# The chunked scan of a hybrid diffusion block: X and Y of a step in four transfers, k k whole, the block inverse in rectangles, the router on column groups

## The chip, the cores and the metric

One Trainium2 chip, one of its cores. The metric is the device time of one execution in microseconds, median of three. All data is fp32.

## The reference

One layer over 1024 latent tokens and 256 context tokens, width 1024. Modulated RMS norm, one input projection, a depthwise convolution, then a token mixer with two head groups, each run forwards and backwards: a gated DeltaNet with 4 heads of 128 x 128 and a Mamba-2 SSD with 8 heads. The context is scanned first, and the latent scan starts from its last state. Then gated norms and the output projection, a second norm, and an expert-choice mixture of 16 SwiGLU experts. The parts that the change touches are these:

```python
# DeltaNet, per chunk
lmat = jnp.where(strict, jnp.einsum("cbhid,cbhjd->cbhij", kb, kc) * decay, 0.0)
uw = lax.linalg.triangular_solve(lmat + jnp.eye(CHUNK, dtype=lmat.dtype), rhs,
                                 left_side=True, lower=True, unit_diagonal=True)
v_new = u_i - jnp.einsum("bhld,bhdv->bhlv", w_i, S)
o = jnp.einsum("bhld,bhdv->bhlv", qg_i, S) + jnp.einsum("bhij,bhjv->bhiv", qk_i, v_new)
S = S * jnp.exp(gl_i)[..., None, None] + jnp.einsum("bhld,bhlv->bhdv", kt_i, v_new)
...
# router of the experts
aff = jax.nn.softmax(jnp.einsum("btd,de->bte", h, router_w).astype(jnp.float32), axis=-1)
gate, idx = lax.top_k(jnp.swapaxes(aff, 1, 2), cap)
```

## The kernel before

Five engines run programs written out by hand, with semaphores between them. In order of time:

- **Projection and convolution** (to about 550 us). 26 blocks of 128 output columns pass through TensorE (L1874) and the convolution on VectorE (L2241). Products k k per tile of 128 tokens go to `kk_dram`, q k to `qk_dram`. The diagonal 32 x 32 blocks of the triangular matrix are inverted in a batch; X (the inverses) and Y (the inverses times beta, transposed) of every tile, head and direction go to `xy_dram`.
- **The scan** (about 555 to 765 us). 20 steps, direction and tile alternating: step s is direction s % 2, n = s // 2; the first four are context steps, the other 16 latent steps. A tile is 128 tokens. In step s every engine works on three steps at once: `own` (s), `nxt` (s + 1) and `two` (s + 2).
- **The merge** (about 772 to 953 us). Eight tiles of 128 tokens: both directions are summed and normed, turned, multiplied with the output projection (L1078), normed again to h2, turned (L1048) and multiplied with the router's weights (`router`, L1057).
- **The choice of rows** (to about 1000 us), then **the experts** (to 1285 us, L1115 and L1134) and the final norm and add.

One step of the scan on TensorE: `from_k(own)`, `block_w(nxt)`, `from_state(own)`, `solve(own)`, `block_vy(nxt)`, `from_chunk(own)` (L495), `outputs(own)` (L468, L469), `block_vp(nxt)`, `to_s(own)`, `to_state(own)`, `block_vq(nxt)`. All seven DeltaNet products but `outputs` go through `per_head` (L411): four heads, 128 x 128 by 128 x 128 each. L484 is `from_state`, L505 `to_state`.

The inverse of the whole 128 x 128 triangle is put together from the four diagonal blocks of X by four of these products, in PSUM bank bA of the direction: W = AT x X, copied to SBUF by ScalarE (L574); P = Y - W x Y on VectorE (`block_p`, L630); Q = W x P, copied by ScalarE; Y += W x Q on VectorE (`block_y`, L635). AT is k k times the decay E, made by VectorE (`block_a`, L625) in place in a buffer per direction, which the load has filled in three rectangles around the diagonal blocks.

VectorE's order in a step: `rest(own)` (L640), `scores(own)` (L686), the mask of E (L606), `y_off` (L670), `block_p(nxt)`, the mask of the SSM decay (L606, wide), `y_diag` (L677), `block_a(two)`, `new_s(own)` (L650), `new_hs(own)` (L662), `block_y(nxt)`. ScalarE's: copy of W, copy of U, exponentials of E (L538), `scaled_x` (L559), copy of Q, exponentials of the SSM decay (L550), copy of the outputs (L600), `tail_k` (L568). GpSimd's: `query_e` (q k x E, L741), `with_eg` (L725, L727), `decayed_hs` (L735), `tail_x` (L748).

SyncE issues all loads of the scan in one order. In step s: `load_at(two)` (L804), `load_xy(two)` (L815), `load_kg(two)` (eg, L822), `load_e(three)` (g, L792), `load_e8(two)` (L830), `load_qk(two)` (L837), `load_kt(two)` (L843), then the store of the outputs of `own` (L889). An issue waits for the buffer that it fills, and all behind it wait too. Behind the scan, SyncE loads the first two tiles of the merge (L979, L982) once GpSimd has made the last product with k (L727).

## Time and profile before

| | |
|---|---|
| median of three executions | 1387.87 us (1385.27 to 1390.42) |
| the profiled execution | 1388.71 us, span 1387.0 us |
| TensorE busy | 1245.3 us, 90% of the span |
| VectorE busy | 764.1 us, 55% |
| ScalarE busy | 430.8 us, 31% |
| GpSimd busy | 220.3 us, 16% |
| mean granted TensorE clock | 0.953 of full speed |

TensorE is PE in the rows, its weight loads PEld, VectorE DVE, ScalarE ACT, GpSimd POOL, SyncE SP. A q behind the name is the engine's queue of DMA issues. Busy time on PE counts a matmul from start to end although the next one has begun; the distance of starts tells what one costs. In brackets behind a row stands the engine's idle time before it and what released it.

### The profile page before, as it was taken

Reading aid. Unit: us, or ns where it says so; the run is one execution under the profiler, and the core shown is the slowest. Engines: PE = TensorE matmul, PEld = TensorE weight load, DVE = VectorE, ACT = ScalarE, POOL = GpSimd, SP = SyncE. Lnnn points to the kernel's source line nnn. Section 1 sums busy time; section 2 is a strip of 40 time slices with the busy share of each in tenths; the row PEclk is TensorE's granted clock in tenths of the full one; section 3 lists DMA queues with packets and bytes.
Section 4 is the critical chain, followed back from the end, with each engine's and each line's share of the span. In section 5 each row is a group of like instructions: output and inputs, shape, how many; then the busy total and the mean of one; then the engine's idle time right before and its main releaser. Section 6 shows DMA issues by size and latency. Waiting matters only on the chain.

```text
span 1387.0 us, 14619 instructions
## 1 busy us (share of the span) xinstructions
PE 1245.3 (90%) x5410; PEld 733.2 (53%) x5410; DVE 764.1 (55%) x1110; ACT 430.8 (31%) x1094; POOL 220.3 (16%) x206
## 2 busy tenths in 40 slices
PE   4999999999999998899999689992199999999983
PEld 3455555455455555889999345552044444444441
DVE  5199889887927776598887446546601101010124
ACT  6233232313111114677786243432011010110122
POOL 0300000010000031266665000000101011010112
PEclk9899999999999999999999799995599999999996
DMA  9823454552052451567676724426479999999967
GB/s 365 265 77 98 125 157 139 158 164 92 17 167 50 106 110 29 149 180 218 206 211 207 260 91 182 181 77 245 149 273 318 350 330 340 333 330 349 320 226 161
DMA packets 207532, 270.69 MB, mean 195 GB/s; under 512 B 75053, under 2 KB 124198, under 8 KB 207462
## 3 DMA queue, kind: packets, MB, share of 16 engines
q1 hardware_dynamic: 187118, 210.97, 46.8%
q0 software_dynamic: 14272, 52.43, 12.6%
q10 hardware_dynamic: 6072, 6.35, 1.3%
q8 instruction: 43, 0.70, 0.2%
q14 instruction: 27, 0.22, 0.1%
HBM read 217.75 MB, written 51.97 MB: 194 GB/s over the span
## 4 chain that ended last, share of the span: by engine, by line
PE 66%; DVE 13%; DMA 10%; ACT 4%; issue 3%; SPq 3%; POOL 0%; POOLq 0%; ACTq 0%; DVEq 0%
PE ps L1874 23%; PE ps L1115 13%; PE ps L411 7%; PE ps L1134 6%; DVE arena L2241 3%; PE ps L1078 2%; DMA y_dram<-arena 2%; DMA arena<-zt_dram 2%; DMA tok_dram<-arena 2%; DMA arena<-ada_w 2%; PE ps L1773 1%; PE ps L495 1%; PE ps L468 1%; PE ps L469 1%; PE ps L1104 1%
## 5 line engine op out<-in xcount | busy, mean ns | idle before, releaser
L1874 PE MATMUL ps<-arena 128*128 128x512 f32 (+1 forms) x1072 | 423.4, 552 | 0.0
L1874 PEld LDWEIGHTS ps<-arena 128*128 128x128 f32 x1072 | 201.3, 190 | 199.5 <-issue 194.4
L1115 PE MATMUL ps<-arena 128*128 128x512 f32 x512 | 226.8, 596 | 1.4 <-ACT arena L1238 1.4
L2241 DVE SCALAR_TENSOR_TENSOR arena<-arena,taps 128x1024 f32<-128x1024 f32 x160 | 209.3, 1308 | 5.5
L1115 PEld LDWEIGHTS ps<-arena 128*128 128x128 f32 x512 | 96.5, 191 | 116.8 <-issue 114.8
L411 PE MATMUL ps<-arena 128*128 128x128 f32 x1080 | 132.2, 277 | 9.7 <-DVE arena L630 4.2
L411 PEld LDWEIGHTS ps<-arena 128*128 128x128 f32 x1080 | 127.2, 192 | 15.8 <-DVE arena L630 5.2
L1401 DVE TENSOR_TENSOR arena<-arena,ps 128x512 f32<-128x512 f32 x16 | 11.0, 688 | 224.1 <-PE ps L1115 224.1
L1078 PE MATMUL ps<-arena 128*128 128x512 f32 x256 | 116.0, 608 | 4.2 <-ACT arena L1187 4.2
L1134 PE MATMUL ps<-arena 128*128 128x512 f32 x256 | 112.8, 593 | 0.0
L1078 PEld LDWEIGHTS ps<-arena 128*128 128x128 f32 x256 | 48.6, 194 | 62.3 <-issue 56.2
L1134 PEld LDWEIGHTS ps<-arena 128*128 128x128 f32 x256 | 47.8, 191 | 55.2 <-issue 55.2
L1258 ACT ACTIVATE arena<-ps 128x512 f32<-128x512 f32 x16 | 9.6, 597 | 198.7 <-PE ps L1115 198.7
L1474 POOL DMA_INDIRECT y_dram<-arena x14 | 22.3, 1593 | 290.5 <-DVE arena L1411 290.5
L2056 ACT ACTIVATE arena<-arena,vcols 128x1280 f32<-128x1280 f32 (+1 forms) x20 | 25.9, 1297 | 136.7 <-DVE arena L2241 136.6
L1238 ACT ACTIVATE arena<-ps 128x512 f32<-128x512 f32 x32 | 19.0, 595 | 144.3 <-PE ps L1104 144.3
L1410 DVE TENSOR_SCALAR arena<-ps,arena 128x512 f32<-128x512 f32 x15 | 11.3, 751 | 91.7 <-PE ps L1134 91.7
L2257 DVE SCALAR_TENSOR_TENSOR arena<-arena,silu_c 128x256 f32<-128x256 f32 x112 | 56.9, 508 | 4.0
L1681 POOL DMA_DIRECT2D arena<-ada_w x16 | 14.5, 906 | 264.5 <-DVE arena L2257 218.0
L574 ACT ACTIVATE arena<-ps 128x512 f32<-128x512 f32 x60 | 35.5, 591 | 51.3 <-PE ps L411 50.8
L606 DVE TENSOR_TENSOR arena<-arena,neg_mask 128x512 f32<-128x512 f32 (+1 forms) x36 | 40.0, 1113 | 5.9 <-DMA arena<-g_dram 5.8
L756 POOL TENSOR_TENSOR arena<-arena,gates 128x1280 f32<-128x1280 f32 x4 | 10.0, 2501 | 205.1 <-DVE arena L2241 185.5
(314 smaller groups left out, 1536.1 us busy)
## 6 DMA issues: line engine op xcount, KB each, us to landing
arena<-exp_w_gate SPq DMA_DIRECT2D x16, 2048.0 KB, 11.0
arena<-exp_w_up SPq DMA_DIRECT2D x16, 2048.0 KB, 9.1
arena<-exp_w_down SPq DMA_DIRECT2D x16, 2048.0 KB, 11.2
arena<-ada_w POOLq DMA_DIRECT2D x16, 1024.0 KB, 6.6
arena<-w_in SPq DMA_DIRECT2D x28, 512.0 KB, 4.7
arena<-ada_w SPq DMA_DIRECT2D x4, 2048.0 KB, 19.9
arena<-x SPq DMA_DIRECT2D x16, 512.0 KB, 6.6
arena<-g_dram SPq DMA_DIRECT2D x16, 512.0 KB, 6.2
```

Source lines behind the costliest of these rows:

```text
L411: last = mm(out[:, h * P:(h + 1) * P], lhsT[:, h, :], rhs[:, h, :], start=True, stop=True)
L574: a(flat(dst), src[:], ACT.Copy).then_inc(sem(name), 1)
L606: return nc.vector.tensor_tensor(out, out, bh(neg_mask[:, d, :], n), ALU.add)
L1078: last = mm(ps[2 + 2 * s + h][:], mixT[s][:, k, :], wo[:, k, h * 512:(h + 1) * 512], start=(k == 0), stop=(k == KD - 1))
L1115: last = mm(ps[gu_bank[s] + j][:], xsT[s][:, k, :], ew[s][j][:, k, :], start=(k == 0), stop=(k == KD - 1))
L1134: last = mm(ps[4 + h][:], hidT[s][:, k, :], ew[s][2][:, k, h * 512:(h + 1) * 512], start=(k == 0), stop=(k == KF - 1))
L1238: a(xsT[e % 2][:, 4 * h:4 * h + 4, :], heads(ps[0][:]), ACT.Copy).then_inc(sem("xsT"), 1)
L1474: p.indirect_dma_start(y_dram, bass.IndirectOffsetOnAxis(ap=idxT[:, e:e + 1], axis=0), ye[e % 2], None, compute_op=ALU.add).then_inc(sem(" ...
L1874: last = mm(ps[3 * (m % 2) + gi][:, 0:w], wring[(m + 1) % NW][:, k, :], hT[:, k, o:o + w], start=(k == 0), stop=(k == KD - 1))
L2056: ins = a(dst, cacc[n_conv(mm) % 2][:, 0:w], ACT.Silu, bias=bcol)
L2241: ins = v.scalar_tensor_tensor(accg, cin_l[ci % 2][:, j // 3:j // 3 + GR, j % 3:j % 3 + GW], tp[:, j:j + 1], accg, ALU.mult, ALU.add)
L2257: ins = v.scalar_tensor_tensor(out, blk[:, k, :], silu_c[:, k, 0:1], out, ALU.mult, ALU.add)
```

## The change

**X and Y.** `xy_dram` is laid out by direction, tile and then X or Y. A step's X and Y come in four transfers (one for each block row) in place of eight.

**k k.** The whole product of a tile (128 x 512) is loaded in one transfer into one buffer KK, shared by all steps. `block_a` multiplies it with E in three rectangles, writing AT. AT is never filled by a load any more. The load for a step waits until the multiply of the step before has read KK.

**The inverse in rectangles.** W, Q and the last product are made, copied and added only in the rectangle where they are not zero: W of direction 1 in rows 0 to 95 and columns 32 to 127, Q in rows 0 to 95 and one half of the columns, the last product in 64 rows and 64 columns. The contraction leaves out rows in which W is zero. Direction 0's W stays whole.

**The router on column groups.** The router's weights, padded to 32 columns a block, are stationary, the transposed h2 moves, and block k writes to rows 32 (k % 4) on, so four sums of two blocks each stand in one bank; the first sum is put in the middle of the first half of the output projection. ScalarE copies them (`logit_parts`), and one matmul with a folded identity adds them (`router_sum`). VectorE builds the padded weights and the folded identity at the start of the merge.

The diff, cut to its core:

```diff
-    xy_dram = dram("xy_dram", (2, 2, NT, DN_H, NB, BL * BL))
+    xy_dram = dram("xy_dram", (2, NT, 2, DN_H, NB, BL * BL))
...
+        KK = zero
...
+        HI, TOP = slice(P // 2, P), slice(0, P - BL)
+        W_R = ((slice(0, P), slice(0, P)), (TOP, slice(BL, P)))
+        Q_R = ((TOP, HI), (TOP, slice(0, P // 2)))
+        Y_R = ((slice(0, P // 2), HI), (HI, slice(0, P // 2)))
...
+            def in_region(d, rc, lhsT, rhs, k=slice(0, P)):
+
+                rows, cc = rc
+                for h in range(DN_H):
+                    last = mm(heads(bA[d][:])[rows, h, cc], lhsT[k, h, rows], rhs[k, h, cc], start=True, stop=True)
+                return last
...
-                per_head(bA[d], AT[d], Xd[d]).then_inc(sem("s_blk"), 1)
+                in_region(d, W_R[d], AT[d], Xd[d]).then_inc(sem("s_blk"), 1)
...
-                per_head(bA[d], W[d], Yd[d]).then_inc(sem("s_blk"), 1)
+                in_region(d, (slice(0, P), slice(0, P)), W[d], Yd[d], W_R[d][0]).then_inc(sem("s_blk"), 1)
...
-                per_head(bA[d], W[d], Y[d]).then_inc(sem("s_blk"), 1)
+                in_region(d, Q_R[d], W[d], Y[d], W_R[d][0]).then_inc(sem("s_blk"), 1)
...
-                per_head(bA[d], W[d], Q[d]).then_inc(sem("s_blk"), 1)
+                in_region(d, Y_R[d], W[d], Q[d], TOP).then_inc(sem("s_blk"), 1)
...
             def block_a(step):
                 d, n = step
-                dve.wait_ge(sem(f"ld_at{d}"), 48 * (n + 1))
+                dve.wait_ge(sem("ld_kk"), 16 * turn(d, n + 1))
                 dve.wait_ge(sem("s_ee"), turn(d, n + 1))
-                v.tensor_tensor(AT[d], AT[d], e_of(step), ALU.mult).then_inc(sem("s_at"), 1)
+                if n > 0:
+                    dve.wait_ge(sem("s_blk"), part(4, (d, n - 1), 1))
+                else:
+                    dve.wait_ge(sem("zero"), 3 + DN_H)
+                kk, e = heads(KK), e_of(step)
+                for b in range(NB - 1):
+                    rows = slice(BL * (b + d), BL * (b + d + 1))
+                    cc = slice(BL * (b + 1), P) if d == 0 else slice(0, BL * (b + 1))
+                    last = v.tensor_tensor(AT[d][rows, :, cc], kk[rows, :, cc], e[rows, :, cc], ALU.mult)
+                last.then_inc(sem("s_at"), 1)
...
+                y_ = region(Y[d], Y_R[d])
+                v.tensor_tensor(y_, y_, region(heads(bA[d][:]), Y_R[d]), ALU.add).then_inc(sem("s_py"), 1)
...
+            p.memset(W[1][:, :, 0:BL], 0.0).then_inc(sem("zero"), 1)
...
+            def load_kk(step):
+                d, n = step
+                if step != steps[0]:
+                    sp_.wait_ge(sem("s_at"), turn(d, n + 1) - 1)
+                sp_.dma_start(KK, kk_dram[tile_of(step)]).then_inc(sem("ld_kk"), 16)
...
-                for dst, x_ in ((Xd[d], 0), (Yd[d], 1)):
-                    xy = xy_dram[d, x_, t].rearrange("h b (j i) -> b j h i", i=BL)
-                    for b in range(NB):
-                        rows = slice(BL * b, BL * (b + 1))
-                        sp_.dma_start(dst[rows, :, rows], xy[b]).then_inc(sem(f"ld_xy{d}"), 16)
+                src = xy_dram[d, t].rearrange("x h b (j i) -> b j (x h) i", i=BL)
+                for b in range(NB):
+                    rows = slice(BL * b, BL * (b + 1))
+                    sp_.dma_start(XY[d][rows, :, rows], src[b]).then_inc(sem(f"ld_xy{d}"), 16)
...
-            load_at(steps[0])
-            load_at(steps[1])
+            sp_.wait_ge(sem("aux"), AUX[("late", 3, 0)] + 1)
+            load_kk(steps[0])
...
             load_xy(steps[1])
+            load_kk(steps[1])
...
-                    load_at(two)
+                    load_kk(two)
                     load_xy(two)
...
                 for k in range(KD):
-                    last = mm(ps[1][:, 0:E_N], h2T[s][:, k, :], rw[:, k, :], start=(k == 0), stop=(k == KD - 1))
+                    rows = slice(BL * (k % NB), BL * (k % NB + 1))
+                    last = mm(ps[1][rows, 0:P], rwide[:, k, :], h2T[s][:, k, :], start=(k < NB), stop=(k >= KD - NB))
                 last.then_inc(sem("logit"), 1)
+
+            def router_sum(t):
+                pe.wait_ge(sem("lparts"), t + 1)
+                mm(ps[1][:, P:P + E_N], lparts[t % 2], fold2[:, 0:E_N], start=True, stop=True).then_inc(sem("lsum"), 1)
...
+            def logit_parts(t):
+                act.wait_ge(sem("logit"), t + 1)
+                if t >= 2:
+                    act.wait_ge(sem("lsum"), t - 1)
+                a(lparts[t % 2], ps[1][:, 0:P], ACT.Copy).then_inc(sem("lparts"), 1)
...
+            v.memset(rwide[:, :, E_N:BL], 0.0)
+            v.tensor_copy(rwide[:, :, 0:E_N], rw[:])
+            link(v.tensor_tensor(fold2, ident[:, 0:BL], ident[:, BL:2 * BL], ALU.add))
+            for q in range(2, NB):
+                link(v.tensor_tensor(fold2, fold2, ident[:, q * BL:(q + 1) * BL], ALU.add))
```

ScalarE's copies of W and Q take the same rectangles, and the stores into `xy_dram` follow its new layout.

## Rows read from the trace of the kernel before

**Rows 1.** The page: busy tenths and granted clock in 40 slices.
```profile
PE   4999999999999998899999689992199999999983
PEclk9899999999999999999999799995599999999996
```
**Rows 2.** Busy time by stretch (PE, PEld, DVE, ACT, POOL, clock, DMA): context, 14 latent steps.
```profile
555.00:594.00 39.00, 32.86 (x258) 30.70 (x256) 22.45 (x35) 24.41 (x67) 12.19 (x10) 1.00 0.62 167
...
599.81:755.60 155.79, 155.55 (x1571) 148.44 (x1570) 131.68 (x211) 121.88 (x391) 96.40 (x69) 1.00 0.66 200
```
**Rows 3.** TensorE's timeline in one latent step: start, duration, line, shapes.
```profile
661.79 2.02 PE L411 MATMUL ps<-arena 128*128 128x128 f32 x16
663.74 1.15 PE L495 MATMUL ps<-arena 128*64 128x64 f32 x32
...
666.71 1.95 PE L411 MATMUL ps<-arena 128*128 128x128 f32 x16
668.50 1.03 PE L505 MATMUL ps<-arena 128*128 128x256 f32 x4
669.37 2.84 PE L411 MATMUL ps<-arena 128*128 128x128 f32 x24
...
672.96 2.02 PE L411 MATMUL ps<-arena 128*128 128x128 f32 x16
```
**Rows 4.** Who waited for whom, 600 to 755 us: total, times, longest.
```profile
POOL arena L741 <- DMA arena<-qk_dram: 48.5, 13, 5.3
...
DVE arena L662 <- POOL arena L735: 10.1, 11, 1.2
```
**Rows 5.** The context steps: chain of waits, then TensorE's timeline.
```profile
580.17 6.81 DMA arena<-qk_dram
```
```profile
591.37 2.05 PE L411 MATMUL ps<-arena 128*128 128x128 f32 x16 [2.01 <-POOL arena L727]
```
**Rows 6.** Chain of waits at a router product; weight loads by shape.
```profile
926.43 1.69 PE ps L1057 x16
```
```profile
L411 PEld LDWEIGHTS ps<-arena 128*128 128x128 f32 x1080 | 127.2, 192 | 15.8 <-DVE arena L630 5.2 <-issue 4.7 <-POOL arena L727 2.2
...
L495 PEld LDWEIGHTS ps<-arena 128*64 128x64 f32 x512 | 16.3, 138 | 2.5 <-issue 0.9
```
**Rows 7.** VectorE's timeline: the multiply before the scan and in it.
```profile
545.15 0.69 DVE L625 TENSOR_TENSOR arena<-arena 128x512 f32<-128x512 f32 x1
...
667.43 1.26 DVE L625 TENSOR_TENSOR arena<-arena 128x512 f32<-128x512 f32 x1 [1.05 <-DMA arena<-kk_dram]
...
678.61 1.25 DVE L625 TENSOR_TENSOR arena<-arena 128x512 f32<-128x512 f32 x1 [1.06 <-DMA arena<-kk_dram]
```
**Rows 8.** SyncE's queue of issues in one latent step.
```profile
668.13 0.43 SPq L837 DMA_DIRECT2D arena<-qk_dram  x1
...
671.24 0.32 SPq L889 DMA_DIRECT2D scan_dram<-arena  x1
671.61 2.13 SPq L804 DMA_DIRECT2D arena<-kk_dram  x3
673.78 4.62 SPq L815 DMA_DIRECT2D arena<-xy_dram  x8
```
**Rows 9.** DMA issues: count, size, median us to landing; then q k's.
```profile
arena<-kt_dram SPq DMA_DIRECT2D x18, 256.0 KB, 6.6
```
```profile
DMA to landing us min/median/max: 3.2/6.5/8.1
```
**Rows 10.** The end of the scan: GpSimd's and VectorE's timelines.
```profile
753.66 2.13 POOL L727 TENSOR_TENSOR arena<-arena 128x512 f32<-128x512 f32 x1
```
```profile
772.25 0.19 DVE L1277 TENSOR_TENSOR mods<-mods,vcols 128x32 f32<-128x32 f32 x1 [9.14 <-DMA scan_dram<-arena]
```
**Rows 11.** Chain of waits in the merge: a middle tile, the last router product.
```profile
836.72 6.13 DMA arena<-zt_dram
...
949.13 3.61 PE ps L1057 x16
```

More of the change, by code:

```diff
@@ L400, in pe_first @@
             pe.wait_ge(sem("s_at"), 1)
-            pe.wait_ge(sem("ld_xy0"), 128)
+            pe.wait_ge(sem("ld_xy0"), 64)
             for h in range(DN_H):
@@ L581, in act_scan @@
                     d, n = nxt
-                    evac(bA[d], W[d], nxt, ("s_blk", part(4, nxt, 1)), "s_wq")
+                    evac(region(heads(bA[d][:]), W_R[d]), region(W[d], W_R[d]), nxt, ("s_blk", part(4, nxt, 1)), "s_wq")
                 if own:
                     d, n = own
-                    evac(bB[d], U[d], own, ("s_xr", turn(d, n + 1)), "s_u")
+                    evac(heads(bB[d][:]), U[d], own, ("s_xr", turn(d, n + 1)), "s_u")
                 if own and two:
@@ L591, in act_scan @@
                     d, n = nxt
-                    evac(bA[d], Q[d], nxt, ("s_blk", part(4, nxt, 3)), "s_wq")
+                    evac(region(heads(bA[d][:]), Q_R[d]), region(Q[d], Q_R[d]), nxt, ("s_blk", part(4, nxt, 3)), "s_wq")
                 if lat(nxt):
@@ L634, in block_y @@
                 dve.wait_ge(sem("s_blk"), part(4, step, 4))
-                v.tensor_tensor(Y[d], Y[d], heads(bA[d][:]), ALU.add).then_inc(sem("s_py"), 1)
+                y_ = region(Y[d], Y_R[d])
+                v.tensor_tensor(y_, y_, region(heads(bA[d][:]), Y_R[d]), ALU.add).then_inc(sem("s_py"), 1)
             def rest(step):
@@ L793, in load_e @@
                     .then_inc(sem(f"ld_e{d}"), 16)
-            def load_at(step):
+            def load_kk(step):
                 d, n = step
-                t = tile_of(step)
-                if n > 0:
-                    sp_.wait_ge(sem("s_blk"), part(4, (d, n - 1), 1))
-                kk = kk_dram[t].rearrange("p (h n) -> p h n", h=DN_H)
-                for b in range(NB - 1):
-                    rows = slice(BL * (b + d), BL * (b + d + 1))
-                    cc = slice(BL * (b + 1), P) if d == 0 else slice(0, BL * (b + 1))
-                    sp_.dma_start(AT[d][rows, :, cc], kk[rows, :, cc]).then_inc(sem(f"ld_at{d}"), 16)
+                if step != steps[0]:
+                    sp_.wait_ge(sem("s_at"), turn(d, n + 1) - 1)
+                sp_.dma_start(KK, kk_dram[tile_of(step)]).then_inc(sem("ld_kk"), 16)
             def load_xy(step):
@@ L922, in hybrid_block @@
         lmax = take(NL)
+        rwide = take(KD * BL).rearrange("p (k n) -> p k n", k=KD)
+        lparts = [take(P) for _ in range(2)]
+        fold2 = take(BL)
         at[0] = 0
@@ L1079, in pe_tail @@
                                   start=(k == 0), stop=(k == KD - 1))
-                    if h == 0 and t >= 2:
-                        router(t - 2)
+                        if h == 0 and k == 3 and t >= 2:
+                            router(t - 2)
+                        if h == 1 and k == 3 and t >= 2:
+                            router_sum(t - 2)
                 last.then_inc(sem("mps"), 1)
@@ L1085, in pe_tail @@
                 router(t)
+                router_sum(t)
             pe.wait_ge(sem("route"), 2)
@@ L1227, in act_tail @@
                     back_sum(t - 1)
+                if t >= 2:
+                    logit_parts(t - 2)
+                if 1 <= t <= NL:
                     back_x2(t - 1)
```

17 lines of the change are left out of this document (10 added, 7 removed).

## The prediction

> **What bounds the kernel now.** I read the page's slices first, to find the stages, then busy time by stretch, then each engine's timeline over one step of the scan, then the chain of waits on both sides of it. The slices [rows 1] show TensorE nearly full and at full clock from the second slice to about 770 us; the clock falls only around 770 us and from 940 to 1000 us. The change touches two places: the scan (555 to 765 us) and the merge with the router (772 to 953 us).
>
> In the latent part of the scan TensorE is the bound: busy 155.55 of 155.79 us in fourteen steps [rows 2], 11.13 us each. A step on TensorE's timeline [rows 3], from 661.79 to 672.96 us, is 56 instructions of the per-head helper (an fp32 matmul is two), 32 of the chunk product, 16 of the outputs and eight wide ones, back to back. Two gaps come from it: 128 moving columns cost (668.50 - 666.71)/16 = 112 ns each, 256 columns (669.37 - 668.50)/4 = 218 ns, so 0.83 ns a column plus 6. But others are close behind [rows 4]: GpSimd idles 48.5 us on the load of q k, VectorE 10.1 us on GpSimd, and about 1.05 us a step on the load of k k [rows 7]. Walking the step, new_hs ends some 0.4 us before TensorE asks for it, and the solve has about 0.1 us to spare behind the same GpSimd work. So a shorter TensorE step is worth its full amount only if q k lands earlier too.
>
> The four context steps are different: TensorE is busy 32.86 of 39 us [rows 2], and the chain of waits runs through SyncE's queue, eight issues of X and Y, the G load behind them, the q k load at 580.17, and GpSimd, until from_k starts after 2.01 us of idle at 591.37 [rows 5].
>
> **The inverse in rectangles.** It removes columns of W (direction 1), P, and Q. P's product has 96 stationary and 64 moving columns, the last product 64 and 64, W of direction 1 96 and 96. What is the gap of such a pair? Moving columns alone give 58 ns at 64 and 85 at 96. But the router's old matmuls, 128 stationary and 16 moving, still take 1.69/16 = 106 ns [rows 6]: there the weight load sets the gap. Its duration is 192 ns at 128 columns and 138 at 64 [rows 6], 0.84 ns a column, so I take 106 - 27 = 79 ns at 96 and 52 at 64. The larger of the two sides gives P 79, the last product 58, W 85. Savings: 8 x (112 - 79) = 0.26 us, 8 x 54 = 0.43 us, 8 x 27 = 0.22 us. Direction 0 gains 0.69 us a step, direction 1 0.91. The first step's inverse is serial and then waits for the G load, so it counts nothing: 9 x 0.69 + 10 x 0.69 + 9 x 0.22 = **15.1 us**. Bounds: if 96 weight columns cost as 128 do, P gains 0.05 us instead of 0.26 and the total is 11.1; if weights don't count at these widths, P gains 0.43 and the total is 18.3.
>
> The Trainium skill ("TensorE: Matmul & The Clock Gate", part 3, The mechanism) says that a weight load overlaps a running matmul only when it targets another row group. All the rectangles use the same row groups, so by that rule nothing overlaps. The trace disagrees: serial, 128 columns would take at least 106 + 106 ns and take 112. The same page (LDWEIGHTS) gives P/1.2 ns for P stationary columns, 80 ns at 96 and 53 at 64; by it the sum would be 15 us, mine.
>
> ScalarE's copies shrink too (W by a quarter in direction 1, Q by half), and VectorE's last add falls from 128x512 to 64x256: about 0.25 us each, off the path in the latent steps.
>
> **k k whole, and the multiply in three.** AT = k k x E was one VectorE instruction on 512 columns, 0.68 us alone and 1.25 us when GpSimd works beside it [rows 7]. Now it is three of 384, 256 and 128 columns. At 0.6 us of work for 512 columns plus 0.06 to 0.15 us an instruction that is 1.1 to 1.25 us alone, up to 2.0 beside GpSimd. With the 0.27 us that the last add gives back, VectorE gets 0.2 to 0.5 us more on some 9.4 of 11.13 us [rows 2]. I expect 9.7 of 10.35: it fits, with the waits inside it. I charge **1.0 us** over the scan; bounds 0 and 0.45 us a latent step, 7 us.
>
> The wait is new: there is one k k buffer, so a load goes out only once the multiply before it is done. On SyncE it stands behind the output store, which goes out after the outputs' copy; at that moment the multiply has long ended (668.70 against 671.61) [rows 7, 8]. So the semaphore costs nothing in a latent step; the bytes may. Before, three issues took from 671.61 to 673.75 and the multiply started at 678.61 after 1.06 us of idle. Now one issue of 0.43 us moves 256 KB right behind the store's 512 KB. The nearest rows are kt, of the same 256 KB, median 6.6 us to landing, and q k, 3.2 to 8.1 us [rows 9]. VectorE gets to the multiply some 5.5 us after the issue and has about 1.5 us of reserve before the next solve. So landing below 7 us costs nothing, and I take 5.5. In the context steps the round trip (0.43 + about 4 + 1.2 us) stays under the step of 7.4 us. At the start the second k k waits for the first multiply (545.15 + 1.2 us) and goes out behind X and Y at about 548, well before its use some 9 us after the first multiply: nothing.
>
> **X and Y in four.** An issue costs about 0.49 us on SyncE's queue whatever its shape: eight take from 673.78 to 678.45 [rows 8]. Four fewer, and two k k issues fewer, take 3.3 to 4 us from SyncE in every step. Everything behind (eg, G, the G of the SSM heads, q k) goes out earlier. q k waits for the outputs of its direction, behind which the next block starts at 666.71 [rows 3], and was issued at 668.13 only because the queue was behind, so it gains 1.1 us there, and more in landing since 512 KB before it have already moved. GpSimd's chain thus stays ahead of a TensorE step 0.8 us shorter. That is what lets the 15.1 us count. The context part gains the stalls: 2.0 us at 591.37 [rows 5], 0.2 right behind it, and 0.3 in the steps before, where VectorE's mask of G stood ahead of P: **2.5 us**; bounds 1 and 4.
>
> **Behind the scan** the tail's loads (4 MB) start when GpSimd's last k multiply ends at 755.8, and the merge starts 16.4 us later [rows 10]. q k earlier moves that multiply some 1 us more than TensorE's end: **1.0 us**; bounds 0 and 2.5.
>
> **The router.** On four column groups, 32 stationary columns each, sixteen instructions should take about 0.6 us: the chunk product on two groups takes 1.15 us for 32 [rows 3]. It adds a ScalarE copy (0.3 us), one matmul for the fold and the hops between. In the middle tiles the path is the load of z transposed, VectorE and ScalarE [rows 11], and TensorE waits: nothing. On the last tiles it is on the path: 926.43, 1.69 us become 0.6 + 0.2, saves 0.9; 949.13, 3.61 us at half clock become about 1.15 + 0.5 (copy) + 0.65 (fold) + 0.2, saves 1.1. Against it VectorE builds the padded router weights and the fold before the first tile, five small instructions of 0.19 to 0.23 us [rows 10], 1.05 us on the path. Net **1.0 us**; bounds -1 and 2. The new store layout of X and Y moves the same rows of 4 KB: nothing.
>
> **Sum.** 15.1 - 1.0 + 2.5 + 1.0 + 1.0 = 18.6 us. The profiled execution took 1388.71 us (span 1387.0); less 18.6 is 1370.1. The median of the three runs is 0.84 lower, so I predict **1369.3 us**.
>
> **Rivals.**
> - *VectorE or GpSimd becomes the bound.* For it: VectorE was busy or waiting on GpSimd nearly all of a step, and the multiply runs beside GpSimd. Against it: 2.2 us of its idle go when q k and k k land earlier. A latent step of about 10.8 us: 16 x 0.45 = 7 us back, 1376.5 us.
> - *Wide weights hold P.* The 96-column load costs as 128: 4 us back, 1373.5. Its opposite, no weight limit: 1366.
> - *Slower: k k lands late.* One buffer, the load can't start before the store's wait is over. It begins to cost at 7 us from issue to landing, and each us more is a us on every one of the 16 latent steps. Half a per cent slower needs (18.6 + 6.9)/16 = 1.6 us more, 8.6 us; at 9 us it is 32 us against the 18.6, 1401 us. For it: q k, of the same size, has landed as late as 8.1 us [rows 9]. Against it: that was behind 1.3 MB issued within 2 us, k k stands behind 0.75 MB.
> - *Little or nothing.* From a step's outputs over q k, GpSimd, new_hs, the last add and the solve to the outputs two steps on is a ring of two steps, 22.3 us with 0.1 to spare. If q k lands no earlier, only the smaller add shortens it: 21.9 us, 10.95 a step, 0.6 x 16 = 9.6 us back, 1378.9. With a costlier multiply in the same ring, as in the first rival, it passes 1381.
>
> **How the numbers follow.** Forecast 0.58, its own range 1366 to 1373; VectorE or GpSimd the bound 0.17; weights otherwise, outside that range, 0.12; little or nothing 0.08; late k k 0.05. The range runs from all low costs together but one (1361) to the little-or-nothing case (1379.5). Half a per cent, 6.9 us, is about what tells a change from none here: below 1381 it is faster, 0.87, within 0.08, slower 0.05.
>
> **What would show it.** Right: a latent step of 10.2 to 10.5 us with TensorE still full; blocks of the last product at 0.46 us; the load of q k no longer what GpSimd waits longest for; from_k of the first latent step without idle; four issues in 2 us. Wrong: VectorE idle on k k over 1.5 us a step; TensorE idle on VectorE before P or the solve; the P block still 0.9 us.

## The result, and the profile after

The changed kernel takes 1394.48 us (median of 11 runs, 1392.55 to 1399.37) against 1389.65 us (11 runs of the kernel before beside it, 1382.93 to 1392.97). The ratio is 1.0038 with a 95% interval of 1.0022 to 1.0054: 5 us slower, where 18.6 us faster was forecast. The profiled execution has a span of 1392.6 us and a granted clock of 0.951. Of all the executions in this document one, of kernel 10, ran at a lower granted clock (0.914) and took 1420.43 us; it is left out of the median there.

I split the difference of 5.6 us between the two spans at four marks that both traces have: the start of the first P on VectorE, of the last from_state on TensorE, of VectorE's first instruction of the merge, and of its search for the largest logit.

| mark (us) | before | after | step longer by |
|---|---|---|---|
| first P | 553.7 | 559.5 | +5.8 |
| last from_state | 759.0 | 766.4 | +1.6 |
| merge starts | 772.3 | 779.1 | -0.6 |
| largest logit | 953.0 | 959.2 | -0.6 |

Behind the last mark the changed kernel is 0.6 us shorter. So the net loss is what was lost ahead of the scan, and the scan itself, where 16.6 us were to come from, is 1.6 us longer.

**Ahead of the scan.** Busy time by stretch, one stretch over the stores of X and Y and the next: the last two columns are the DMA engines' busy share and GB/s. First the kernel before, then the changed one.
```profile
380.00:385.00 5.00, 5.00 (x13) 2.24 (x12) 1.69 (x3) 0.00 (x0) 0.00 (x0) 1.00 0.53 166
385.00:390.00 5.00, 5.00 (x19) 2.58 (x18) 0.00 (x0) 2.17 (x4) 0.00 (x0) 1.00 1.02 339
```
```profile
380.00:385.00 5.00, 5.00 (x13) 2.18 (x12) 1.25 (x3) 0.00 (x0) 0.00 (x0) 1.00 0.27 48
385.00:390.00 5.00, 5.00 (x19) 2.64 (x18) 0.00 (x0) 2.17 (x4) 0.00 (x0) 1.00 0.50 181
```
And of the changed kernel the chain of waits, then who waited for whom from 400 to 470 us on TensorE.
```profile
390.03 20.11 DMA arena<-w_in
```
```profile
PE ps L1924 <- DMA arena<-w_in: 4.9, 1, 4.9
```
The same eight stores, of the same bytes, keep the DMA engines half as busy. The first load of projection weights is issued behind them, takes 20.11 us to land, and TensorE stands still for 4.9 us. The kernel before has no such wait: it reached the same projection with its weights in place. From the issue of the first of these stores to the first P it is 178.4 us in the changed kernel and 172.1 before. Over all the traces of this case it is 172.0 to 173.6 us in the eight kernels with the old layout and 178.4 to 179.2 in the five with the new one (kernel 12, which cuts some stores up, stands apart), so the layout costs 6 to 7 us.

**A latent step.** TensorE's timeline of the changed kernel over one step, which answers to [rows 3].
```profile
661.21 0.81 PE L441 MATMUL ps<-arena 128*96 128x64 f32 x8
661.87 1.11 PE L422 MATMUL ps<-arena 128*128 128x128 f32 x8
662.81 1.03 PE L525 MATMUL ps<-arena 128*128 128x256 f32 x4
663.77 0.68 PE L441 MATMUL ps<-arena 96*64 96x64 f32 x8
664.38 1.16 PE L422 MATMUL ps<-arena 128*128 128x128 f32 x8
665.37 0.84 PE L441 MATMUL ps<-arena 128*96 128x96 f32 x8
666.05 1.06 PE L504 MATMUL ps<-arena 128*128 128x256 f32 x4
667.53 1.13 PE L422 MATMUL ps<-arena 128*128 128x128 f32 x8 [0.42 <-DVE arena L670]
```
Read the distances of starts, not the durations. P's product takes 661.87 - 661.21 = 0.66 us for eight, 82 ns each (79 forecast). W of direction 1 takes 666.05 - 665.37 = 0.68, 85 ns (85 forecast). The last product takes 664.38 - 663.77 = 0.61, 76 ns (58 forecast), and the full-width block behind it 0.99 instead of the 0.90 of eight at 112 ns. The four wide ones ahead of it (L525, before L505) take 663.77 - 662.81 = 0.96 us where they took 0.87 [rows 3]. The last line is new: TensorE waits on VectorE.

Over 120 us of the latent part, busy time of PE, PEld, DVE, ACT and POOL: before, then after.
```profile
620.00:740.00 120.00, 119.98 (x1201) 114.42 (x1198) 99.53 (x162) 94.70 (x304) 76.09 (x55) 1.00 0.70 211
```
```profile
620.00:740.00 120.00, 113.35 (x1186) 104.03 (x1185) 118.93 (x179) 89.35 (x296) 77.89 (x53) 1.00 0.73 218
```
The bound has changed hands. TensorE was full and has 6.65 us of idle now; VectorE is full. The mean distance of thirteen latent steps, from from_state to from_state, went from 11.12 to 11.34 us; some steps take 10.6, others 12.3.

Where TensorE idles tells what holds it. Its waits in this window, then its timeline at one of them:
```profile
PE ps L515 <- issue: 5.3, 7, 1.0
```
```profile
681.36 1.15 PE L515 MATMUL ps<-arena 128*64 128x64 f32 x32 [0.73 <-issue]
```
The profile names no releaser, but L515 is the chunk product, which waits for VectorE's scores (L716). In each of its eight waits in this window it starts 0.10 us after the second scores product has ended. So 5.4 of TensorE's 6.65 us of idle are a wait for the scores.

What fills VectorE stands in its instructions by shape in the same window (busy us, mean ns of one, idle before). Before, then after:
```profile
L686 DVE TENSOR_TENSOR arena<-arena 128x512 f32<-128x512 f32 x22 | 14.2, 684 | 0.0
L625 DVE TENSOR_TENSOR arena<-arena 128x512 f32<-128x512 f32 x11 | 13.5, 1228 | 7.2 <-DMA arena<-kk_dram 7.2
...
L606 DVE TENSOR_TENSOR arena<-arena,neg_mask 128x512 f32<-128x512 f32 x10 | 6.8, 685 | 0.0
```
```profile
L716 DVE TENSOR_TENSOR arena<-arena 128x512 f32<-128x512 f32 x22 | 28.7, 1342 | 0.0
L626 DVE TENSOR_TENSOR arena<-arena,neg_mask 128x512 f32<-128x512 f32 x11 | 15.8, 1433 | 0.0
...
L659 DVE TENSOR_TENSOR arena<-arena,ps 128x512 f32<-128x512 f32 x11 | 7.4, 672 | 0.0
...
L653 DVE TENSOR_TENSOR arena<-arena 32x384 f32<-32x384 f32 x10 | 6.0, 596 | 0.1
L653 DVE TENSOR_TENSOR arena<-arena 32x256 f32<-32x256 f32 x10 | 5.1, 514 | 0.1
L665 DVE TENSOR_TENSOR arena<-arena,ps 64x256 f32<-64x256 f32 x11 | 4.6, 414 | 0.2
L653 DVE TENSOR_TENSOR arena<-arena 32x128 f32<-32x128 f32 x10 | 3.6, 357 | 0.2
```
The multiply in three (1.47 us) is hardly dearer than the one was (1.23). The scores (L716, before L686) and the narrow mask (L626, before L606), which the change doesn't touch, take twice as long: 1342 and 1433 ns against 684 and 685. An instruction of the same size with one operand from PSUM (L659) keeps its 672. The two timelines show it; VectorE's, then GpSimd's:
```profile
677.77 0.69 DVE L670 TENSOR_TENSOR arena<-arena,ps 128x512 f32<-128x512 f32 x1
678.38 2.88 DVE L716 TENSOR_TENSOR arena<-arena 128x512 f32<-128x512 f32 x2
681.18 1.52 DVE L626 TENSOR_TENSOR arena<-arena,neg_mask 128x512 f32<-128x512 f32 x1
682.63 0.68 DVE L700 TENSOR_TENSOR arena<-ps,eG 128x512 f32<-128x512 f32 x1
```
```profile
677.76 1.28 POOL L755 TENSOR_TENSOR arena<-arena 128x512 f32<-128x512 f32 x1
679.11 1.59 POOL L757 TENSOR_TENSOR arena<-arena 128x512 f32<-128x512 f32 x1
680.67 1.49 POOL L765 TENSOR_TENSOR arena<-arena,eGt 128x512 f32<-128x512 f32 x1
682.12 1.49 POOL L778 TENSOR_TENSOR arena<-arena,wtail 128x512 f32<-128x512 f32 x1
```
In these rows a VectorE instruction with both operands in SBUF takes about as long as the GpSimd product beside it (1.44 and 1.52 us against 1.28 to 1.59); those with one operand from PSUM keep their 0.68 and 0.69 us. That is contention, not work: run 3 below, which takes GpSimd's work away, brings the scores back to 693 and the narrow mask to 700 ns. The Trainium skill ("SBUF — State Buffer", Who interferes with whom) says that a VectorE instruction with two SBUF inputs contends with a GpSimd instruction that reads SBUF, while one with at most one SBUF input does not. The rows agree with it on both sides.

**Queue and loads.** SyncE's queue of issues in a latent step answers to [rows 8]; under it the DMA issues of the scan (count, KB, median us to landing), which answer to [rows 9].
```profile
666.52 0.43 SPq L830 DMA_DIRECT2D arena<-kk_dram  x1
666.99 2.36 SPq L840 DMA_DIRECT2D arena<-xy_dram  x4
...
672.64 0.32 SPq L862 DMA_DIRECT2D arena<-qk_dram  x1
```
```profile
arena<-kk_dram SPq DMA_DIRECT2D x14, 256.0 KB, 3.6
...
arena<-qk_dram SPq DMA_DIRECT2D x14, 256.0 KB, 3.9
```
k k whole lands in 3.6 us, X and Y go out in 2.36, and q k is issued 0.2 us behind the outputs (672.45) instead of 1.4, and lands in 3.9. This part did what was forecast, but for one sign: GpSimd still waits longest for the load of q k, 46.3 us between 620 and 740 (before: 41.2), since its issue waits for the outputs.

**The scan's end and the merge.** GpSimd's last k product, VectorE's first instruction of the merge [rows 10], and the chain at a middle and at the last router product [rows 11]:
```profile
758.33 2.49 POOL L757 TENSOR_TENSOR arena<-arena 128x512 f32<-128x512 f32 x1
```
```profile
779.09 0.19 DVE L1322 TENSOR_TENSOR mods<-mods,vcols 128x32 f32<-128x32 f32 x1 [8.58 <-DMA scan_dram<-arena]
```
```profile
931.50 0.57 PE ps L1086 x16
...
939.13 0.13 PE ps L1091 x2
...
956.84 1.12 PE ps L1086 x16
...
958.32 0.62 PE ps L1091 x2
```
The merge starts 18.3 us behind GpSimd's last product (16.4 before). A router product costs 0.57 + 0.13 us instead of 1.69, the last one 2.1 from first matmul to fold instead of 3.61.

### The profile page after: what moved, and what is told of

It reads as the page before. It is cut to its first block, busy times and chain, and to the rows that moved or that the text cites. A ratio compares the mean times of both kernels' runs of the same rounds, so it can differ in the third digit from the quotient of the medians.

```text
span 1392.6 us, 14592 instructions
## 1 busy us (share of the span) xinstructions
PE 1235.7 (89%) x5426; PEld 711.5 (51%) x5426; DVE 792.7 (57%) x1155; ACT 426.7 (31%) x1102; POOL 226.0 (16%) x207
## 4 chain that ended last, share of the span: by engine, by line
PE 53%; DVE 25%; DMA 9%; ACT 5%; issue 5%; SPq 2%; POOLq 0%; DVEq 0%; ACTq 0%
PE ps L1924 21%; PE ps L1151 13%; PE ps L1170 6%; DVE arena L626 3%; DVE arena L716 3%; PE ps L1111 2%; DMA y_dram<-arena 2%; DVE arena L2291 2%; DMA arena<-ada_w 2%; DVE arena L2362 1%; DVE arena L2360 1%; DMA arena<-w_in 1%; DMA arena<-zt_dram 1%; PE ps L1823 1%; PE ps L441 1%
## 5 line engine op out<-in xcount | busy, mean ns | idle before, releaser
L1924 PEld LDWEIGHTS ps<-arena 128*128 128x128 f32 x1072 | 201.9, 191 | 206.1 <-issue 195.9
L1151 PEld LDWEIGHTS ps<-arena 128*128 128x128 f32 x512 | 96.7, 192 | 117.2 <-issue 115.1
L1111 PEld LDWEIGHTS ps<-arena 128*128 128x128 f32 x256 | 47.9, 194 | 60.0 <-issue 54.0
L441 PE MATMUL ps<-arena 128*128 128x128 f32 (+5 forms) x632 | 71.2, 257 | 6.8 <-DVE arena L659 3.9
L1170 PEld LDWEIGHTS ps<-arena 128*128 128x128 f32 x256 | 48.1, 192 | 55.6 <-issue 55.6
L441 PEld LDWEIGHTS ps<-arena 128*128 128x128 f32 (+4 forms) x632 | 64.0, 172 | 14.4 <-issue 7.8
L1303 ACT ACTIVATE arena<-ps 128x512 f32<-128x512 f32 x16 | 9.6, 598 | 199.2 <-PE ps L1151 199.2
L422 PE MATMUL ps<-arena 128*128 128x128 f32 x448 | 63.5, 285 | 3.2 <-DVE arena L670 2.6
L1283 ACT ACTIVATE arena<-ps 128x512 f32<-128x512 f32 x32 | 19.0, 594 | 144.3 <-PE ps L1140 144.3
L422 PEld LDWEIGHTS ps<-arena 128*128 128x128 f32 x448 | 55.9, 194 | 8.0 <-DVE arena L665 3.5
L626 DVE TENSOR_TENSOR arena<-arena,neg_mask 128x512 f32<-128x512 f32 (+1 forms) x36 | 48.4, 1346 | 2.6 <-DMA arena<-g_dram 2.6
## 6 DMA issues: line engine op xcount, KB each, us to landing
arena<-exp_w_gate SPq DMA_DIRECT2D x16, 2048.0 KB, 11.1
```

Source lines behind the costliest of these rows:

```text
L422: last = mm(out[:, h * P:(h + 1) * P], lhsT[:, h, :], rhs[:, h, :], start=True, stop=True)
L441: last = mm(heads(bA[d][:])[rows, h, cc], lhsT[k, h, rows], rhs[k, h, cc], start=True, stop=True)
L626: return nc.vector.tensor_tensor(out, out, bh(neg_mask[:, d, :], n), ALU.add)
L1111: last = mm(ps[2 + 2 * s + h][:], mixT[s][:, k, :], wo[:, k, h * 512:(h + 1) * 512], start=(k == 0), stop=(k == KD - 1))
L1151: last = mm(ps[gu_bank[s] + j][:], xsT[s][:, k, :], ew[s][j][:, k, :], start=(k == 0), stop=(k == KD - 1))
L1170: last = mm(ps[4 + h][:], hidT[s][:, k, :], ew[s][2][:, k, h * 512:(h + 1) * 512], start=(k == 0), stop=(k == KF - 1))
```

## The experiments

Each was run against the kernel before on the same chip. "Step" is the mean distance of thirteen latent steps (before: 11.12 us), VectorE's and TensorE's busy time is of the 120 us from 620 to 740. Times of different runs come from different chips, so each is compared with the kernel before beside it.

**1. The old store layout in the changed kernel** (with it X and Y need eight loads again)
```diff
-xy_dram = dram("xy_dram", (2, NT, 2, DN_H, NB, BL * BL))
+xy_dram = dram("xy_dram", (2, 2, NT, DN_H, NB, BL * BL))
```


> The changed kernel with X and Y as before: the old layout of xy_dram, stores of 128 rows at one stride, eight loads a step. Theory A (the new store layout is slow and holds up the load of w_in behind it, and in the scan VectorE and GpSimd bound each other): the load of w_in that landed 20.1 us after 390.03 lands in about 14, the scan starts 5 to 6 us earlier, and the latent steps stay near 11.4 us, since the four issues are not what makes them long: about 1388 us. Rival B (four transfers in place of eight moved q k early, and that shifted GpSimd onto VectorE's SBUF work): the latent steps fall to 11.1 us or less as well, about 1384. Rival C (the late start comes from elsewhere): the start of the scan does not move, 1394.

1391.98 us, ratio 1.0024 (1.0002 to 1.0046). The first P starts at 551.4, 8 us earlier (of which 1.7 lie ahead of the stores), and the stall on w_in is gone. But the step is 11.41 us and VectorE busy 118.84. The layout costs its microseconds ahead of the scan, and X and Y in four have nothing to do with the long steps.

**2. query_e held back until P's copy is there**
```diff
                 pool.wait_ge(sem("s_ee"), turn(d, n + 1))
+                pool.wait_ge(sem("s_py"), part(2, step, 1))
```


> The changed kernel, but GpSimd's q k times E of the next step waits until VectorE has written P of that step, so that GpSimd's five products begin about 4 us later in the step, beside VectorE's reads of PSUM and not beside the scores and the narrow mask. Theory A (contention between the two on SBUF, by phase): the scores fall from 1.35 us each to 0.75, the narrow mask from 1.47 to 0.75, latent steps to 10.6 to 10.8 us, in all 8 to 12 us faster than the changed kernel, about 1384. Rival D (VectorE has simply too much to do with three multiplies): the steps stay at 11.3 to 11.4 us, and the contention only moves to other instructions; a wait more makes it rather slower, 1394 to 1397.

1396.52 us, ratio 1.0069 (1.0045 to 1.0094); step 11.14. VectorE by shape:
```profile
L653 DVE TENSOR_TENSOR arena<-arena 32x256 f32<-32x256 f32 x11 | 15.4, 1398 | 0.1
L716 DVE TENSOR_TENSOR arena<-arena 128x512 f32<-128x512 f32 x22 | 14.1, 682 | 0.0
L653 DVE TENSOR_TENSOR arena<-arena 32x384 f32<-32x384 f32 x11 | 13.8, 1258 | 0.1
...
L653 DVE TENSOR_TENSOR arena<-arena 32x128 f32<-32x128 f32 x10 | 9.6, 956 | 0.2
```
Scores and narrow mask are back at 682 and 683 ns, and the three multiplies take 3.61 us in their place. VectorE is as full as without this wait (118.92). The contention moved and didn't go away: Rival D's account, not Theory A's.

**3. GpSimd almost without work.** Four of its five products of a step (q E, q and k with exp(G), the state's decay) cut to 4 or 2 columns a head; their results are not computed.
```diff
-                p.tensor_tensor(QE[d], QE[d], e_of(step), ALU.mult)
+                p.tensor_tensor(QE[d][:, :, 0:4], QE[d][:, :, 0:4], e_of(step)[:, :, 0:4], ALU.mult)
```


> The changed kernel with four of GpSimd's five products in a scan step (q k times E, q and k times the decay, the decayed SSM state) cut to 16 elements a partition, so that they leave out nearly all of their work; the output is not the reference's. Theory A: VectorE's instructions return to their times alone (scores 0.65 us, narrow mask 0.68, three multiplies 1.1 in all), TensorE sets the latent step, 10.3 to 10.5 us, 1380 us. Rival D: the steps stay above 11 us.

1384.55 us (one execution), span 1382.2.
```profile
620.00:740.00 120.00, 120.00 (x1267) 111.69 (x1268) 99.61 (x191) 95.19 (x312) 29.09 (x56) 1.00 0.76 233
```
Without GpSimd in its way VectorE needs 99.61 of 120 us, scores and narrow mask take 693 and 700 ns, three multiplies 0.55 + 0.42 + 0.28 us, and TensorE is full again at 10.65 us a step. Two numbers follow. VectorE's own work is 99.61/120 x 10.65 = 8.8 us a step; of the 118.93/120 x 11.34 = 11.2 us that it is busy in the changed kernel the other 2.4 are contention. And the rectangles can give TensorE little: its steps are 10.79 and 10.55 us in turn, where the shortest of the kernel before are 11.04, so 0.25 and 0.49 us. (The means, 11.12 and 10.65, differ by 0.47, but 0.08 of that is waiting in the kernel before.)

**4. The rectangles alone**, on the kernel before
```diff
-                per_head(bA[d], W[d], Y[d]).then_inc(sem("s_blk"), 1)
+                in_region(d, Q_R[d], W[d], Y[d], W_R[d][0]).then_inc(sem("s_blk"), 1)
...
-                per_head(bA[d], W[d], Q[d]).then_inc(sem("s_blk"), 1)
+                in_region(d, Y_R[d], W[d], Q[d], TOP).then_inc(sem("s_blk"), 1)
```

> The kernel before with the rectangles of the inverse alone: loads, the multiply by E and the router as before. If the two-step ring over q k, GpSimd, VectorE and the solve binds once TensorE is shorter, a latent step falls only from 11.15 to 10.9 us, 3 to 6 us in all with the context steps, 1384 to 1387 us. If TensorE is the only bound, 10.4 us a step and 1375.

1386.45 us, ratio 0.9976 (0.9961 to 0.9992): 3 us faster. Step 10.90, VectorE busy 97.90 with 7.5 us idle on k k and 10.8 on GpSimd. That is what the last of the rivals in the prediction gives for a q k that lands no earlier (10.95): here, with the loads as before, not only TensorE sets the step.

**5. k k whole and the three multiplies alone**
```diff
-                v.tensor_tensor(AT[d], AT[d], e_of(step), ALU.mult).then_inc(sem("s_at"), 1)
+                for b in range(NB - 1):
...
+                    last = v.tensor_tensor(AT[d][rows, :, cc], kk[rows, :, cc], e[rows, :, cc], ALU.mult)
```


> The kernel before with k k loaded whole into the one buffer and multiplied in three instructions, nothing else. Theory A (VectorE and GpSimd share the way to SBUF, and the change gives VectorE three instructions of two SBUF operands in place of one while nothing gets shorter): the three together take 2.0 us or more where one took 1.16, VectorE's idle time in the latent steps goes from 20 to under 8 us, and a latent step is 11.2 to 11.4 us; 1 to 4 us slower than before, 1391 to 1393. Rival E (k k early is a gain, since VectorE waited 1.05 us a step for it): the step stays at 11.15, TensorE full, no change, 1389.

1400.52 us, ratio 1.0062 (1.0043 to 1.0082). Step 11.95, VectorE busy 119.05, scores 1408 ns and narrow mask 1560. It does on the kernel before what it does in the changed one, and costs 1400.52 - 1390.87 = 9.7 us, where Theory A had 1 to 4.

**6. The store layout alone**, X and Y still loaded in eight
```diff
-sp_.dma_start(xy_dram[d, x_, 0:NL].rearrange("t h b f -> (t h b) f"), lat)
+sp_.dma_start(xy_dram[d, 0:NL, x_].rearrange("t h b f -> t (h b) f"), lat)
```

> The kernel before with the new layout of xy_dram alone; eight loads a step as before, from the new places. Theory A: the stores of 8 x 16 rows go out over fewer DMA engines than 128 rows at one stride, the five loads of w_in behind them land late, TensorE waits for them 5 us at about 405 us, and the whole kernel is 5 to 6 us slower, 1394 to 1396; the latent steps stay 11.15 us. Rival C: the start of the scan does not move and the time is that of before, 1389.

1398.4 us, ratio 1.005 (1.0031 to 1.0068). The wait for w_in is 4.9 us again, the step 11.09: Theory A, and 7.5 us rather than its 5 to 6.

**7. The changed kernel without its k k edit**
```diff
-                sp_.dma_start(KK, kk_dram[tile_of(step)]).then_inc(sem("ld_kk"), 16)
+                    sp_.dma_start(AT[d][rows, :, cc], kk[rows, :, cc]).then_inc(sem(f"ld_at{d}"), 16)
...
-                    last = v.tensor_tensor(AT[d][rows, :, cc], kk[rows, :, cc], e[rows, :, cc], ALU.mult)
+                v.tensor_tensor(AT[d], AT[d], e_of(step), ALU.mult).then_inc(sem("s_at"), 1)
```

> The changed kernel with k k as before: three rectangles loaded into AT, one multiply. Theory A: VectorE has idle time again (over 8 us in 120), the latent step falls from 11.4 to 10.8 or 10.9 us, as with the rectangles alone, 7 to 9 us less than the changed kernel, 1386 to 1388 with the slow stores still in it. Rival F (the early q k that the four transfers bring is what puts GpSimd onto the scores and the narrow mask): the scores still take over 1.2 us each, the step stays above 11.2 us, 1392 to 1395.

1384.28 us, ratio 0.9953 (0.993 to 0.9976); step 10.72. That is 6.6 us faster than the kernel before beside it, where the changed kernel is 4.8 slower: 11.4 us between them (10.2 by the bare medians).
```profile
620.00:740.00 120.00, 119.70 (x1247) 110.84 (x1247) 109.59 (x169) 95.44 (x311) 86.31 (x56) 1.00 0.69 218
```
TensorE is full. VectorE is still hindered (narrow mask 1310 ns) but has room for it. The scores, which TensorE waited for, are back at 773 ns: rival F fell.

**8. The rectangles on the kernel before, one multiply of 96 columns, and the tail's second load behind the last two stores**
```diff
-                v.tensor_tensor(AT[d], AT[d], e_of(step), ALU.mult).then_inc(sem("s_at"), 1)
+                v.tensor_tensor(AT[d][:, :, cc], AT[d][:, :, cc], e_of(step)[:, :, cc], ALU.mult).then_inc(sem("s_at"), 1)
...
             load(0)
-            load(1)
             for step in steps[-2:]:
                 scan_store(sp_, step)
+            load(1)
```


> The kernel before with the rectangles of the inverse, the one multiply narrowed to the 96 columns that its rectangles cover (0.46 us alone in place of 0.60), and behind the scan the loads of the merge's second tile issued after the last two stores and not before them. Theory A: the multiply gives VectorE 0.15 to 0.3 us a step, the step is 10.7 to 10.8 us; the last store, which stood 7 us in the queue behind 4 MB, lands 2 to 3 us sooner, and the merge starts that much earlier: 1381 to 1384 us, 6 us under before. If the end of the scan is not set by that queue, only 1385 to 1386 as with the rectangles alone.

1379.6 us, ratio 0.9924 (0.9896 to 0.9951). Step 10.82; the merge starts 761.5 - 756.2 = 5.3 us behind TensorE's last outputs instead of 8.3. The multiply of 96 columns gave little (1131 ns against 1205 in run 4, a step of 10.82 against 10.90); the load order gave more: from the last from_state to the merge it is 10.3 us against 14.7 in run 4.

**9. Three multiplies alone**, on the rectangles loaded as before
```diff
-                v.tensor_tensor(AT[d], AT[d], e_of(step), ALU.mult)
+                    last = v.tensor_tensor(AT[d][rows, :, cc], AT[d][rows, :, cc], e[rows, :, cc], ALU.mult)
```


> The kernel before with one edit: the multiply by E in three instructions, one for each 32-row rectangle, on the rectangles that the loads have filled; k k is loaded as before. Theory A (splitting the multiply is most of what k k whole costs: the three instructions hold VectorE 1.3 to 1.6 us beside GpSimd, against 1.25 for one): a latent step of 11.4 to 11.7 us, the kernel at 1396 to 1401. Rival B (the cost comes with the whole load: k k there 4 us earlier lets VectorE and GpSimd meet in each step): step 11.1 to 11.2, the kernel at 1389 to 1392.

1397.05 us, ratio 1.0067 (1.0041 to 1.0092), step 11.72.
```profile
L629 DVE TENSOR_TENSOR arena<-arena 32x256 f32<-32x256 f32 x10 | 12.3, 1230 | 0.1
...
L629 DVE TENSOR_TENSOR arena<-arena 32x384 f32<-32x384 f32 x10 | 10.9, 1092 | 0.7 <-DMA arena<-kk_dram 0.6
...
L629 DVE TENSOR_TENSOR arena<-arena 32x128 f32<-32x128 f32 x10 | 7.9, 787 | 1.0 <-DMA arena<-kk_dram 0.8
```
The loads are those of the kernel before, and nearly the whole loss is there (8.2 us against the 9.7 of run 5): 3.11 us of multiplies against 1.23. Splitting is the cost, not k k whole. Theory A holds in the step and the time, though it had the multiplies at 1.3 to 1.6 us; rival B fell.

**10. The router alone**, on the kernel before
```diff
-                    last = mm(ps[1][:, 0:E_N], h2T[s][:, k, :], rw[:, k, :], start=(k == 0), stop=(k == KD - 1))
+                    last = mm(ps[1][rows, 0:P], rwide[:, k, :], h2T[s][:, k, :], start=(k < NB), stop=(k >= KD - NB))
```

> The kernel before with the router on column groups alone. Theory A (the merge ran 1 to 3 us shorter in the kernels that have it): start of the merge to the largest logit 178 to 180 us against 180.7, the kernel at 1387.5 to 1389.5. Rival B (the copies and the folding matmul give it all back): 1389 to 1392, with TensorE's share of weight loads between the last logits and the softmax shorter but the same span.

1385.99 us, ratio 0.9982 (0.9968 to 0.9996). From the merge's start to the largest logit 179.8 us against 180.7. A gain of 0.6 to 4.4 us by the times, 0.9 by the trace.

**11. Kernel 8 with the router**

> Rectangles, one multiply of 96 columns, the tail's second load behind the last two stores (the fastest so far, 1379.6), and the router on column groups. Theory A (the router's saving is its own and adds): 1377 to 1379. Rival B (no gain of the router): 1379 to 1381, merge as long as in the kernel without it, 181.8 us.

1379.52 us, ratio 0.9923 (0.9906 to 0.9941): the same as kernel 8 within both intervals. Its merge takes 180.4 us against 181.8, so the trace has 1.4 us for the router; the times can't tell them apart. One trace against another says little here: this stretch is 180.5 to 184.2 us in the six kernels with the old router (mean 182.3) and 179.8 to 183.4 in the eight with the new one (mean 180.8). The means differ by 1.4 us.

**12. Kernel 7, the load order and narrow multiply of kernel 8, and the context stores in two**
```diff
-    sp_.dma_start(xy_dram[d, NL:NT, x_].rearrange("t h b f -> t (h b) f"), ctx_)
+    for i in range(NT - NL):
+        sp_.dma_start(xy_dram[d, NL + i, x_].rearrange("h b f -> (h b) f"),
+                      ctx_[i * DN_H * NB:(i + 1) * DN_H * NB])
```


> The changed kernel without its k k edit, with one multiply of 96 columns, the tail's second load behind the last two stores, and each of the four context stores of X and Y (outer dimension 2) cut into two stores of sixteen rows of 4 KB; the latent stores keep their outer dimension of 8. Theory A (the stores with a short outer dimension run on few engines, the two-row ones worst): the wait for w_in falls from 4.9 us to under 2, the first P starts 3 to 5 us earlier than at 559.9, the kernel at 1376 to 1379. Rival B (the scattered destination costs in any form, or the latent stores alone hold w_in): w_in still waited for by 4 to 7 us, first P at 559 to 561, the kernel at 1380 to 1382 by the load order alone.

1374.53 us, ratio 0.9892 (0.987 to 0.9914): 15 us faster than the kernel before, below what either theory said.
```profile
L1923 PE MATMUL ps<-arena 128*128 128x512 f32 (+1 forms) x1072 | 424.5, 554 | 2.1 <-DMA arena<-w_in 2.1
```
TensorE's wait for w_in fell to 2.1 us (5.0 in kernel 7) and the first P starts at 554.9, 5.0 us earlier. Of these 1.6 us lie ahead of the stores; from the first store to the first P it is 175.5 us, where kernel 7 has 179.0 and the old layout some 172.3. So cutting the two-row stores gave back 3.5 of 6.7 us, and the form of the store is what costs; the latent stores, still with eight rows outermost, may hold the rest. The Trainium skill ("DMA: Bandwidth & Descriptors", Why a DMA increments its semaphore by 16 and not by 1) says that a transfer is split over the largest number of engines up to 16 that divides the outermost dimensions of both sides. By it the old stores (128 and 32 rows outermost) would run on 16 engines, the new ones on 8 and 2. The DMA share in the rows above, 0.50 where it was 1.02, agrees. The traces also record every increment on the semaphore that these stores raise: 128 for the eight stores of the kernel before, 16 each, but 48 in the changed kernel and 164 for the twelve of run 12. If the cut context stores have 16 each again, the other four have (164 - 8 x 16)/4 = 9 each, and the two-row stores (48 - 4 x 9)/4 = 3. That is 8 and 2 with one more for each store, which fits the engine counts worked out above. The last increment comes at 408.4 us in the changed kernel, at 392.2 before and at 403.9 in run 12.

## Why the prediction was wrong

The forecast was 1370.1 us for the profiled execution; the one taken needs some 5 us more than before. The terms, in the order of the sum:

- **Rectangles, 15.1 us: mis-sized, and mostly never reached.** W at 85 ns was right and P, 82 for 79, nearly. The last product was 76 ns and not 58, and the full-width instructions around a narrow block pay. In the median of the latent steps, where eight full-width products take 0.89 us elsewhere, they take 0.95 behind P and 1.00 behind the last product, and the four wide ones ahead of the last product 0.96 and not 0.87. Why they do is not shown. With that P and the last product save 0.24 - 0.05 + 0.29 - 0.10 - 0.09 = 0.29 us a step instead of 0.69, and W of direction 1 another 0.22 - 0.03 = 0.19 (the four wide ones behind it pay 0.03). Over the same nineteen and nine steps it is 19 x 0.29 + 9 x 0.19 = 7.2 us, under my lower bound of 11.1. Run 3 shows the same from the other end, steps 0.25 and 0.49 us shorter in turn; run 4 has 3 us for the rectangles alone. The step that failed put the two loads of a pair side by side and took the larger, without asking what stands before and behind the block.
- **The multiply in three, 1.0 us: the term that lost the case.** "I expect 9.7 of 10.35: it fits" failed. Alone, the three take 1.24 us (run 3), inside my 1.1 to 1.25. Beside GpSimd they take 3.11 (run 9) or 3.61 (run 2), where I had bounded them at 2.0. Where they escape that, as in the changed kernel, the scores and the masks pay. And it was by the scores that TensorE then waited, 5.4 of its 6.65 us of idle in 120. I priced the edit as VectorE's work and took the slow-down from one row, 1.25 against 0.68 us [rows 7], as a property of that one instruction. In these runs it hit every kind of VectorE instruction with two SBUF operands in the step: masks, scores and multiplies. Alone these need 1.22 + 0.68 + 2 x 0.68 + 1.24 = 4.5 us a step (masks, scores, multiply), GpSimd's five products about 3 x 1.27 + 2 x 1.04 = 5.9 (each kernel's shortest rows). Were they to take strict turns they would need 10.4 of 10.65 us. With one multiply of 0.68 it is 9.8. That the lack of slack is why the step breaks is argued from this sum; that the split costs 8 to 11 us is shown (9.7 in run 5, 11.4 in run 7, 8.2 in run 9).
- **k k's landing, nothing: right.** 3.6 us against 5.5 expected, and no wait of VectorE on it. The slower rival fell: the kernel is slower, but not by it.
- **X and Y in four: right on the queue.** 2.36 us for four, q k 1.2 us nearer its outputs. From the first P to the first from_state it is 37.5 us instead of 39.6, 2.1 gained for the 2.5 forecast; from_k of the first latent step still waits 0.64 us, now for VectorE. What I took for pure gain, a GpSimd that starts earlier in the step, also puts its products beside other instructions of VectorE.
- **Behind the scan, 1.0 us: 0.6.** The merge starts 12.7 us after the last from_state and not 13.3, a difference that two traces can't tell from none (run 10, with the scan and its end as before, has 13.5, run 6 has 15.0). GpSimd's last product did move earlier against TensorE, by 2.4 us; the loads between took 1.8 of it back.
- **The router, 1.0 us: right** within what can be told: 0.6 us here, 0.9 alone, 1.4 in run 11 and in the means of all traces, with 1.0 saved at a middle tile and 1.5 at the last.
- **The store layout, "moves the same rows of 4 KB: nothing": wrong by 6 to 7 us.** Run 6 alone costs 0.5%, and from the stores to the first P it is 6.3 us more in the changed kernel. I looked at bytes and row size and not at the shape of the transfer, nor at who is queued behind it.

Of the rivals, the first named the mechanism, VectorE with GpSimd as the bound, and had it at 10.8 us a step: the size was off by 0.5 us a step, and its 1376.5 us by 18. Together: 18.6 forecast; less 6.3 for the layout, 7.9 for the rectangles, 10.4 for the multiply (11.4 from run 7, less the 1.0 charged) and 0.4 each for the context steps, the scan's end and the router leaves -7.2, against -4.8 measured. The terms aren't known to better than that: the interval of run 7 alone is 3 us to either side.

Two readings of the prediction are wrong without bearing on this. Eight issues from 673.78 to 678.45 are 0.58 us each and not 0.49, and [rows 8] has issues of 0.32 to 0.71 us, so an issue's cost isn't the same for all shapes. And 0.83 ns a column plus 6 gives 59 ns at 64 columns, not 58.

Open: the strict-turns sum above wasn't tried by itself; why full-width instructions pay beside a narrow block; and the new layout with all stores on full width, since the remaining 2.1 us of wait in kernel 12 may be the latent stores.

## What to carry to other kernels

Price an edit on VectorE with what GpSimd does at that moment: count the instructions of both that read two operands from SBUF, and treat their sum, not VectorE's share, as the load; cutting one such instruction into three smaller ones cost 8 to 11 us, about half of what the whole change was to bring. A transfer's cost isn't its bytes: when a DRAM layout changes, look at the outermost dimension of every store and load that touches it and at the load queued behind. Price a narrow matmul from a whole step, with its neighbours: here the blocks before and behind took back 0.24 of the 0.53 us that P and the last product saved.

## What was not expected of the hardware

- A store of the same rows of 4 KB, outermost dimension 8 or 2 instead of 128 or 32, ran at 48 and 181 GB/s where it ran at 166 and 339, and held up the next load on the queue for 20.11 us. Cutting the two-row stores in two gave back 3.5 us.
- Three VectorE products of 768 columns in all on 32 partitions took 3.1 to 3.6 us beside GpSimd and 1.24 alone, while one of 512 columns on 128 partitions took 1.23 beside it and 0.69 alone [rows 7].
- A pair of 64 stationary and 64 moving columns takes 76 ns, not much less than one of 96 and 64 (82). The block of eight 128-wide products behind it takes 0.10 us longer, and the four 256-wide ones before it 0.09.
